# An encoder trunk on one core: the first input projection fed in four stages of 256 features instead of two of 512, and two pieces of VectorE's work moved

## What is computed

```
mod = silu(c) @ ada_w[layer] + ada_b[layer]            # 6 x 1024: shift, scale, gate (mixer and ffn)
h = rms_norm(x, norm_mix_g[layer]) * (1.0 + sc_m) + sh_m
proj = h @ w_in[layer]                                 # 256 x 2304: qa, ka, va, qd, kd, vd
... rotary embedding, window attention with a sink, differential attention ...
lam = exp(sum(lq1 * lk1)) - exp(sum(lq2 * lk2)) + lambda_init
x = x + g_m * (concat(ya, yd) @ w_out[layer])
```

## Time and profile before

| what | us |
|---|---|
| median of three executions (1649.42 to 1651.68) | 1650.8 |
| the profiled execution, its own time | 1651.28 |
| span of the profiled execution | 1649.5 |
| TensorE matmul busy | 1604.1 (97%) |
| VectorE busy | 1286.6 (78%) |
| ScalarE busy | 1018.0 (62%) |
| mean granted clock of TensorE | 0.996 of full |

### The profile page before, as it was taken

One profiled execution on the slowest core, in us unless ns is written; L12 is line 12 of the kernel. 1 busy time (PEld: TensorE's weight loads), 2 busy tenths in 40 slices (PEclk: granted clock), 3 DMA queues, 4 the chain that ended last, 5 costly groups with the idle time before them and its releaser, 6 DMA issues.

```text
span 1649.5 us, 20834 instructions
## 1 busy us (share of the span) xinstructions
PE 1604.1 (97%) x7979; PEld 1304.7 (79%) x7980; DVE 1286.6 (78%) x934; ACT 1018.0 (62%) x748; POOL 43.8 (3%) x74
## 2 busy tenths in 40 slices
PE   5999999999999999999999999999999999999998
PEld 5857888886767888888888888888888888888886
DVE  4968644554955778988898898888889889888887
ACT  2455433442354567677777767767767777777774
POOL 0011000000001000000000000000000000000002
PEclk9999999999999999999999999999999999999999
DMA  9897694458578289999999999999999999999994
GB/s 354 294 354 253 224 387 153 153 200 310 182 313 308 103 350 403 378 371 387 381 378 385 379 383 380 383 375 387 371 381 390 371 386 384 377 381 387 379 384 158
DMA packets 164051, 546.71 MB, mean 331 GB/s; under 512 B 10106, under 2 KB 12226, under 8 KB 158882
## 3 DMA queue, kind: packets, MB, share of 16 engines
q1 hardware_dynamic: 156818, 528.02, 84.2%
q10 hardware_dynamic: 4800, 11.32, 2.0%
q0 software_dynamic: 2384, 6.70, 1.3%
HBM read 528.18 MB, written 15.73 MB: 330 GB/s over the span
## 4 chain that ended last, share of the span: by engine, by line
PE 83%; DVE 7%; DMA 4%; ACT 3%; issue 2%; SPq 1%; POOL 0%; DVEq 0%; POOLq 0%; ACTq 0%
PE ps L1959 26%; PE ps L1961 25%; PE ps L1960 25%; DVE raw_lo L1515 2%; PE ps L2256 2%; DMA weights<-in_ffn_w_down_dram 1%; PE ps L1885 1%; DVE weights_lo L1138 1%; DMA weights<-in_ada_w_dram 1%; DMA weights<-in_w_in_dram 1%; ACT raw_hi L950 1%; DMA raw<-in_moe_w_down_dram 1%; PE ps L2040 1%; PE ps L2013 1%; PE ps L2025 1%
## 5 line engine op out<-in xcount | busy, mean ns | idle before, releaser
L1515 DVE TENSOR_TENSOR raw_lo<-raw,raw_hi 128x4096 fp32r<-128x4096 f32 x188 | 830.8, 4424 | 135.9 <-ACT raw_hi L950 133.5
L950 ACT ACTIVATE raw_hi<-raw 128x4096 fp32r<-128x4096 f32 x188 | 683.5, 3636 | 212.2 <-PE ps L1961 200.0
L1959 PE MATMUL ps<-raw_hi,hT_hi 128*128 128x512 f32 x1008 | 395.7, 393 | 2.5 <-DVE hT_lo L1730 1.3
L1961 PE MATMUL ps<-raw_hi,hT_lo 128*128 128x512 f32 x1008 | 392.6, 389 | 0.0
L1960 PE MATMUL ps<-raw_lo,hT_hi 128*128 128x512 f32 x1008 | 392.2, 389 | 0.0
L1959 PEld LDWEIGHTS ps<-raw_hi,hT_hi 128*128 128x128 f32 x1008 | 189.3, 188 | 41.4 <-issue 2.0
L1961 PEld LDWEIGHTS ps<-raw_hi,hT_lo 128*128 128x128 f32 x1008 | 189.2, 188 | 39.8
L1960 PEld LDWEIGHTS ps<-raw_lo,hT_hi 128*128 128x128 f32 x1008 | 189.4, 188 | 38.2
L1959 PE MATMUL ps<-raw_hi,m_actT_hi 128*128 128x512 f32 x504 | 197.1, 391 | 0.0
L1961 PE MATMUL ps<-raw_hi,m_actT_lo 128*128 128x512 f32 x504 | 196.4, 390 | 0.0
L1960 PE MATMUL ps<-raw_lo,m_actT_hi 128*128 128x512 f32 x504 | 196.1, 389 | 0.0
(11 more groups left out here) (237 smaller groups left out, 1327.8 us busy)
## 6 DMA issues: line engine op xcount, KB each, us to landing
raw<-in_moe_w_gate_dram SPq DMA_DIRECT2D x126, 1024.0 KB, 6.2
raw<-in_moe_w_up_dram SPq DMA_DIRECT2D x126, 1024.0 KB, 8.4
raw<-in_moe_w_down_dram SPq DMA_DIRECT2D x126, 1024.0 KB, 8.1
weights<-in_ada_w_dram SPq DMA_DIRECT2D x20, 2048.0 KB, 9.7
weights<-in_ffn_w_gate_dram SPq DMA_DIRECT2D x14, 1024.0 KB, 5.8
weights<-in_ffn_w_up_dram SPq DMA_DIRECT2D x14, 1024.0 KB, 8.6
weights<-in_ffn_w_down_dram SPq DMA_DIRECT2D x7, 2048.0 KB, 9.7
weights<-in_w_in_dram SPq DMA_DIRECT2D x6, 2048.0 KB, 12.9
```

The costliest lines, as they stand in the source:

```text
L950: act.activation(raw_hi[HIGH_OF[p]][:], raw[RAW_OF[p]][:], ACT.Copy).then_inc(m_hi, 1)
L1515: dve.tensor_tensor(raw_lo[r][:], raw[r][:], raw_hi[h][:].bitcast(F32), ALU.subtract).then_inc(m_lo, 1)
L1959: pe.matmul(dst, stat_hi, hi, start=start, stop=False, skip_group_check=True)
L1961: return pe.matmul(dst, stat_lo, hi, start=False, stop=stop, skip_group_check=True)
```

## The change

The lead is cut into four stages of 256 features. Chunk n of the modulation now is scale *and* shift of features 256n to 256n+255: two DMAs of 256 columns each, into the two halves of one slot. Each stage is load, chunk, row copy, transpose, bias and A, four copies of 128 x 128 (two feature blocks for two token tiles), high part, low part, and one quarter of the projection. The loads of `w_in` alternate with those of `ada_w`.

```diff
-LEAD = [(s, a) for s in range(2) for a in (1, 0)]
-LEAD_BANK = [(0, 1), (4, 6)]
-LEAD_UNITS = [0, 2, 1, 3]
+LEAD = 4
+LEAD_BANK = [(0, 1, 0), (2, 3, 0), (4, 6, 0), (4, 6, P)]
...
-        put(("ada", 0, n), n % 2, ("ada", n + 1))
+        put(("ada", 0, n), n % 2, ("ada", n + 1), 2)
...
+        def lead_part(a, p):
+
+            return a[:, 2 * p:2 * p + 2, :]
+
+        def lead_tmp(p):
+            return tmp[:, p % 2, :].rearrange("p (k n) -> p k n", k=2)
...
-            s, a = LEAD[n]
-            return (ps[:, LEAD_BANK[s][0], a * P:a * P + P], modrow[:, 0, (2 * a + s) * P:(2 * a + s) * P + P],
-                    ps[:, LEAD_BANK[s][1], a * P:a * P + P])
+            rows, cols, at = LEAD_BANK[n]
+            return ps[:, rows, at:at + P], modrow[:, 0, n * P:n * P + P], ps[:, cols, at:at + P]
...
-                s, a = LEAD[n]
-                at = a * D + 512 * s
-                load(("ada", 0, n), W[:, n % 2, :].rearrange("p (k n) -> p k n", k=KD),
-                     ada_first[:, :, at:at + 512])
+                slot, holder, _ = plan[("ada", 0, n)]
+                free(holder)
+                for a in range(2):
+                    at = a * D + 256 * n
+                    sp.dma_start(W[:, slot, a * PART:a * PART + PART].rearrange("p (k n) -> p k n", k=KD),
+                                 ada_first[:, :, at:at + 256]).then_inc(w_loaded[slot], 16)
...
-            lead_ada(0)
-            lead_ada(1)
-            lead_columns_in(0, 0)
-            lead_columns_in(0, 1)
-            lead_ada(2)
-            lead_columns_in(1, 0)
-            lead_ada(3)
-            lead_columns_in(1, 1)
+            for n in range(LEAD):
+                lead_ada(n)
+                lead_columns_in(n // 2, n % 2)
...
-                    pool.wait_ge(cols_ready, 1)
+                    pool.wait_ge(lead_cols, 1)
                     for dst, src in const_loads:
                         pool.dma_start(dst, src).then_inc(consts_loaded, 16)
```

ScalarE and VectorE, the lead and the places of the moved pieces:

```diff
-            lead_high(0, 0)
-            lead_turned_high(0)
-            lead_high(0, 1)
-            lead_turned_high(1)
-            lead_high(1, 0)
-            lead_turned_high(2)
-            lead_turned_high(3)
-            lead_high(1, 1)
+            for n in range(LEAD):
+                lead_high(n // 2, n % 2)
+                lead_turned_high(n)
+                if n == 1:
+                    act.wait_ge(lam_dot, 1)
+                    act.activation(lame[:], lams[:], ACT.Exp).then_inc(lam_exp, 1)
 
             for c in range(2, IN_CHUNKS):
                 straight("in", 0, c)
                 if c == 3:
                     for dst, src in bias_loads(0, slice(1, 3)):
                         act.dma_start(dst, src).then_inc(bias_loaded, 16)
-            act.wait_ge(lam_dot, 1)
-            act.activation(lame[:], lams[:], ACT.Exp).then_inc(lam_exp, 1)
...
+                two = slice(2 * n, 2 * n + 2)
                 dve.wait_ge(ada_used, n + 1)
-                dve.tensor_copy(block, rows).then_inc(mod_ready if n == 3 else lead_mod, 1)
-                if n == 3:
+                dve.tensor_copy(block, rows).then_inc(mod_ready if n == LEAD - 1 else lead_mod, 1)
+                if n == LEAD - 1:
                     dve.wait_ge(cols_ps, 1)
                 else:
                     dve.wait_ge(lead_turned, n + 1)
-                at = slice(4 * s, 4 * s + 4)
-                b = (5 + a) * KD + 4 * s
-                i = dve.tensor_tensor(modc[:, 0, a, at], cols.rearrange("p (g x) -> p g x", x=32)[:, :, 0],
-                                      vcols[:, b:b + 4], ALU.add)
-                if n == 3:
+                i = dve.tensor_tensor(modc[:, 0, 0:2, two], cols.rearrange("p (a s x) -> p a s x", a=2, s=2)[:, :, :, 0],
+                                      vcols[:, 5 * KD:7 * KD].rearrange("p (a k) -> p a k", a=2)[:, :, two], ALU.add)
+                i.then_inc(lead_cols, 1)
+                dve.wait_ge(lead_cols, n + 1)
+                i = dve.scalar_tensor_tensor(out=A[:, 0, 0, two], in0=modc[:, 0, 1, two], scalar=1.0,
+                                             in1=vcols[:, KD + 2 * n:KD + 2 * n + 2], op0=ALU.add, op1=ALU.mult)
+                if n == LEAD - 1:
                     i.then_inc(cols_ready, 1)
                     dve.wait_ge(cols_ready, 1)
                 else:
                     then(i)
...
-                for kk in range(4):
-                    kd = 4 * q + kk
-                    a = dve.tensor_scalar(tmp_part(p)[:, kk, :], turned_rows(0, i)[:, kk, :], A[:, 0, 0, kd:kd + 1],
-                                          modc[:, 0, 0, kd:kd + 1], ALU.mult, ALU.add)
+                for t in range(NT):
+                    for kk in range(2):
+                        kd = 2 * p + kk
+                        a = dve.tensor_scalar(lead_tmp(p)[:, kk, t * P:t * P + P],
+                                              turned_rows(0, 2 * t + p // 2)[:, kd % 4, :], A[:, 0, 0, kd:kd + 1],
+                                              modc[:, 0, 0, kd:kd + 1], ALU.mult, ALU.add)
...
                     if j < PAIRS:
                         maxima(layer, j)
-                    if j == 0:
+                    if layer == 0 and j == 0:
+                        low_of("out", 0, 0, 0)
+                    if j == 1 - layer:
                         low_of("out", layer, 0, 1)
                     if 1 <= j <= PAIRS:
                         probabilities(layer, j - 1)
...
-            lead_round(0)
-            lead_round(1)
-            lead_copy(0)
-            low_of("in", 0, 0, 0)
-            lead_low(0)
-            lead_copy(1)
-            lead_low(1)
-            low_of("in", 0, 0, 1)
-            lead_round(2)
-            low_of("in", 0, 1, 0)
-            lead_round(3)
-            lead_copy(2)
-            lead_copy(3)
-            lead_low(2)
-            lead_low(3)
-            low_of("in", 0, 1, 1)
+            for n in range(LEAD):
+                lead_round(n)
+                lead_copy(n)
+                low_of("in", 0, n // 2, n % 2)
+                lead_low(n)
+                if n == 1:
+                    differences()
...
-                if layer == 0:
-                    differences()
                 rope(layer, 3, 1)
-                low_of("out", layer, 0, 0)
+                if layer:
+                    low_of("out", layer, 0, 0)
```

TensorE:

```diff
-                if s and a:
+                if n == 2:
                     pe.wait_ge(tr_copied, 2)
                 rows = lead_block(n)[0]
                 for kk in range(KD):
                     for g in range(4):
-                        at = kk * 512 + g * P
+                        at = (g // 2) * PART + kk * 256 + (g % 2) * P
...
-                    pe.wait_ge(tr_lo, 2 * (q // 2) + t + 1)
+                    pe.wait_ge(tr_lo, q + 1)
+                    if q == 0 and t:
+                        pe.wait_ge(lead_cols, 2)
...
-            lead_chunk(0)
             for i in range(TURNS):
                 turn_rows_of(0, i)
+            lead_chunk(0)
             lead_columns(0)
+            keep(18, 2)
             lead_chunk(1)
             lead_columns(1)
-            keep(18, 2)
-            lead_project(0, IN_ORDER[0:3])
+            lead_project(0, IN_ORDER[0:4])
             lead_chunk(2)
-            lead_project(0, IN_ORDER[3:4])
             lead_columns(2)
-            lead_project(1, IN_ORDER[0:2])
+            lead_project(1, IN_ORDER[0:4])
             lead_chunk(3)
             lead_columns(3)
-            lead_project(1, IN_ORDER[2:4])
             lead_project(2, IN_ORDER[0:4])
             lead_project(3, IN_ORDER[0:4])
```

More of the change, by code:

```diff
@@ L171, in plan_ring, with put @@
     loads, holder, plan = [0] * (RING + 2), [None] * (RING + 2), {}
-    def put(name, slot, holds):
-        plan[name] = (slot, holder[slot], loads[slot] + 16)
-        loads[slot] += 16
+    def put(name, slot, holds, dmas=1):
+        plan[name] = (slot, holder[slot], loads[slot] + 16 * dmas)
+        loads[slot] += 16 * dmas
         holder[slot] = holds
@@ L1219, in lead_round @@
                     then(i)
-                if a:
-                    then(dve.scalar_tensor_tensor(out=A[:, 0, 0, at], in0=modc[:, 0, 1, at], scalar=1.0,
-                                                  in1=vcols[:, KD + 4 * s:KD + 4 * s + 4], op0=ALU.add, op1=ALU.mult))
             def lead_copy(p):
-                i = LEAD_UNITS[p]
-                q = i % 2
                 if p == 0:
@@ L1915, in lead_columns @@
                     pe.wait_ge(lead_mod, n + 1)
-                pe.transpose(cols, block, ident[:]).then_inc(cols_ps if n == 3 else lead_turned, 1)
+                pe.transpose(cols, block, ident[:]).then_inc(cols_ps if n == LEAD - 1 else lead_turned, 1)
             def lead_project(q, units):
```

14 lines of the change are left out of this document (5 added, 9 removed).

## The result

The changed kernel takes 1657.3 us (median of 6 runs, 1654.7 to 1658.7), the kernel before beside it 1649.4 (also 6 runs). The recorded ratio of the comparison, with its 95% interval, is 1.0040 [1.0030, 1.0051]; the two medians alone would give 1.0048. In a second comparison (5 runs against 23) it took 1656.3 us against 1650.8, with the same recorded ratio, 1.0040 [1.0026, 1.0054] (medians alone: 1.0034). So it is slower by 0.40%, 6.6 us. The forecast of +3.4 us, 1654.2 us, had the sign and half the size; the range held 1657.3 at its very edge.

The account below looks back on a forecast made before the run. TensorE was taken as the bound, busy 97%, with the lead paced by DMA loads. Lead -3.9 + 3.7 + 1.5 = +1.3, attention +2.1, sum +3.4 us on 1650.8 gave 1654.2 us; range 1649.6 to 1657.3.

Parts of the forecast that it names:

- Structure, -3.9 us: Lead: four stages shorten the chain behind the fourth modulation chunk from 17.4 to 13.5 us, 3.9 us gained.
- 1 KB packets, +3.7 us: Lead loads: 1 KB runs move slower than 2 KB ones, 0.9 us more for each of four chunks, 3.7 us.
- the first rival: Lead: 1 KB packets do not slow the stream; total 1650.5 us, no change that can be measured; chance 0.2.
- Constants, +1.5 us: Lead: POOL's six constant loads now fall among the loads the fourth chunk waits for, 1.5 us later (1.0 to 2.2).
- the second rival: Lead: only part is paid, packets 2.5 us and 0.5 of the constants hidden; total 1652.0 us; chance 0.17.
- 44.5 us for the fourth chunk: Lead: the fourth modulation chunk's load lands at 44.5 us instead of 39.3, from packets 3.7 and constants 1.5.
- Projection, 0: Projection: VectorE loses constants (2.2 us) and a low part (2.28 us), both off the path, so gain 0.
- rival "faster": Projection: VectorE sets the start of attention, so relieving it gains time; total 1646.8 us; chance 0.06.
- SP's extra issues, at nothing: Lead: four more DMA issues of 0.47 us each at most, covered by queued loads, cost 0; uncovered, 1.9 us.
- Attention, +2.1 us: Attention of layer 0: first probabilities slip by one low part, 2.2 us, of which 2.1 us stays.
- The shift at the end differs from that at 140 us: Whole kernel: sign that the forecast is wrong, since any shift was to carry through unchanged from 140 us to the end.

Follow-up runs that it names:

- b2: Kernel before with each of its four lead loads made as two transfers of 256 columns, so runs of 1 KB; ratio 1.0015 to before.
- b3: Kernel before with each of its four lead loads made as two transfers of half the rows, runs staying at 2 KB; ratio 0.9994 to before.
- a3: Changed kernel with the six constant loads, their arithmetic and the exponential back where the kernel before has them; ratio 1.0019 to before.
- b1: Changed kernel with both constants and low parts of the first output chunk back in their old places, the four stages alone; ratio 1.0009 to before.
- a1: Kernel before with only the attention edit: the first w_out chunk's two low parts behind the first and second maxima; ratio 1.0019 to before.
- a4: Changed kernel with 11 identity matmuls, results unused, filling TensorE's wait for E in layer 0; ratio 1.0018 to before.
- b4: b1 with the first output chunk's two low parts moved in layer 0 behind the head outputs of steps 4 and 5; ratio 1.0061 to before.
- b6: b1 with the second low part of the first output chunk moved in layer 0 behind E of pair 0; ratio 1.0016 to before.
- c1: The changed kernel itself measured once more, also called "again"; ratio 1.0040 to before.
- a2: Changed kernel with the two low parts of the first output chunk back where they stood before; ratio 1.0014 to before.
- b5: b1 with layer 0's two low parts moved, the first behind E of pair 0, the second behind the head output of step 3; ratio 1.0003 to before.
- b7: Changed kernel with the second low part of layer 0 moved behind E of pair 0; ratio 1.0018 to before.

## Why the prediction was right, and where it was not

- **Structure, -3.9 us: right to the digit.** The chain behind the fourth chunk is 46.60 to 46.64 us in the four profiles with the old lead, 42.75 to 42.79 in the five with the changed lead and early constants: -3.85. In the changed kernel the 48th matmul behind the last transpose, the end of the fourth quarter, ends at 57.9 us (forecast 58.0). My reading of the fixed chain from the earlier trace rows holds.
- **1 KB packets, +3.7 us: the step that failed most.** At the fourth chunk it is 0.8 (b2 against b3) to 1.7 us. The stretches at 333 and 339 GB/s in the earlier trace rows don't stand for a lead with many loads queued: there, in a3 from 24 to 28 us, nearly all packets are 1 KB and move at 354. That is the first rival's argument, which I had given 0.2; what the runs show lies between it and the second rival, in which 2.5 us are paid.
- **Constants, +1.5 us: mis-sized too, the other way.** Early constants put the third chunk at 35.3 us and the fourth at 45.0 (means of five profiles), late ones at 32.3 and 40.8: 3.1 and 4.2 us. I had taken 1.5 out of 1.0 to 2.2; already the engines' time that POOL's queue had in the changed kernel is 2.2 us. The 1.1 us that come up between third and fourth chunk are mainly the clock, which I had left out here as well: in four of the five profiles the third chunk waited 2.46 to 4.49 us for DMA, ran for 2.87 to 3.60 us in place of 1.95, and the fourth followed without a wait for its load. In the fifth, the changed kernel's first, the fourth chunk waited 1.21 us for its load.
- **So 44.5 us for the fourth chunk against 44.32 is two errors that cancel, luck and not insight:** 5.2 us forecast, 5.9 measured (1.7 + 4.2). With the structure that makes +1.3 forecast, +2.0 measured over the profiles (mean qkT copy at 87.75 in the five with early constants, 85.71 in before, a1 and b3).
- **Projection, 0: right for the changed kernel** (VectorE's last V copy waits 2.05 us, 1.49 before in the earlier trace rows), so the rival "faster" had no ground. But the reserve was shorter than it looked: b1 shows VectorE bound once the lead alone is shortened.
- **SP's extra issues, at nothing: right** (b3 has the fourth chunk at 39.35), though a pair of them took 4.4 to 5.1 us in the changed kernel where I had counted 0.47 us each.
- **Attention, +2.1 us: the wait is right (2.68, slip 2.1), the price is not.** What I left out is the clock. I costed the wait at its length, as though TensorE came out of it as it went in. All four profiles with the 2.68 us wait (changed, again, a1, a3) have the lower clock behind it, and their attention is 1.6, 3.1, 3.0 and 3.1 us above a4's 52.25. Of the others, b4 has it behind waits of its own and b6 at 86 us, behind its wait for V. At the very end of the attention, behind a wait of 1.15 us that all profiles have, it costs 0.1 to 0.5 us in c1, a2, a3, b2 and b6.
- **The sum.** 2.0 + 2.1 + 2.4 (1.6 and 3.1 averaged) = 6.5 us, the 6.6 of the ratio. Of it 2.4 in the attention and 1.1 in the lead are clock, 3.5 us, as much as the slope over the runs gave. With the lead of the changed kernel's own two profiles (+1.03 and +0.26 against 86.04) it is 5.1; that spread of 1.4 us is what single profiles leave open.
- The shift at the end differs from that at 140 us (3.4 against 4.8), which I had named as a sign that I am wrong. It is the stretch at the lower clock near 420 us, which of the two only the profile of before has, and it made the profiled execution look as though the forecast were exact.

## What to carry to other kernels

A wait put into a full TensorE costs its length, and it may cost what the clock takes behind it: price it both ways, and look at the granted clock of the stretch behind it, not at the wait alone. Small loads from another queue are to be priced by the DMA engines' time that their packets take in the trace, not by bytes, and kept out of a stretch where a stream sets the pace. And a forecast that meets one landmark may do so by two errors; the parts have to be run apart before the sum is believed.

## What the runs showed of the hardware

- TensorE's granted clock fell to its lower level (1.2 GHz) behind each wait of 2.68 us in the attention, in 4 of 4 profiles, and behind b4's of 2.17 and 5.17 us (chunks of 2.49 and 3.64 us). It stayed at 1.00 there when the same time was filled with matmuls (a4) or the wait was 1.40 or 1.41 us (b5, b6, b7). The Trainium skill (TensorE: Matmul & The Clock Gate, Part 1) says that a default of 1.2 GHz returns with idleness and that activity lifts it; these rows agree.
- The length of the wait alone does not decide it. The clock fell behind 1.89 us in the lead of the changed kernel (second chunk 3.61 us) and stayed behind 1.88 us in c1 (1.95); it fell behind 2.26 us for V in b6 and stayed at 1.00 behind 2.55 us in b1. What decides is not shown. The chunk behind the 2.68 us took 3.11 us in one profile and 3.64 in three.
- Executions of one kernel differ by such stretches: the kernel before took 1645.6 to 1653.6 us over 91 runs, 1.07 us for each 0.001 of mean clock. A profile's span is one draw from that.
- A packet of POOL's constant loads held a DMA engine for 86 ns in one stretch of the changed kernel and for 232 ns in the next, beside the weights' 83 and 66 ns.
- A chunk at the lower clock need not cost anything: behind the second chunk of the changed kernel (clock 0.54) TensorE still waited 1.44 us for the next load. In c1, a2, a4 and b7 it was the third chunk, with no wait for a load behind it, and there it did cost.
